# Rotations in four operations, and a state space core that gates one token tile per scan step

## What is computed

```python
def mamba2_mixer(u, w_in, ...):
    ...
    y = ssd_chunked_scan(xh * dt[..., None], dt * a, bm, cm)
    y = (y + xh * d_skip[:, None]).reshape(b, l, D_INNER)
    yg = (y * silu(z)).reshape(b, l, SSM_GROUPS, D_INNER // SSM_GROUPS)
    yg = yg * rsqrt(mean(square(yg), axis=-1, keepdims=True) + RMS_EPS)
    return (yg.reshape(b, l, D_INNER) * norm_w) @ w_out
```

```python
def rope(t):
    ...
    t1, t2 = t[..., :half], t[..., half:]
    return concatenate([t1 * cos - t2 * sin, t1 * sin + t2 * cos], axis=-1)
...
q, k, v = rope(hv(q)), rope(hv(k)), hv(v)
q_idx = rope(q_idx.reshape(B, S, IDX_HEADS, IDX_DIM))
k_idx = rope(k_idx[:, :, None, :])[:, :, 0, :]
...
sc = relu(einsum('bqhd,bsd->bqhs', q_idx_block, k_idx))
score = einsum('bqhs,bqh->bqs', sc, w_idx_block) * idx_scale
```

## Time and profile before

| | |
|---|---|
| median of three executions | 2491.34 us |
| lowest and highest | 2490.29, 2491.82 us |
| profiled execution | 2485.71 us |
| its span in the trace | 2484.0 us |
| granted TensorE clock, mean | 0.988 |
| TensorE busy | 2398.8 us, 97% |
| VectorE busy | 996.8 us, 40% |
| ScalarE busy | 636.3 us, 26% |
| GpSimd busy | 1497.5 us, 60% |

### The profile page before, as it was taken

How to read it: one execution, slowest core, us unless ns; L and a number is a source line. 1 busy time by engine, 2 the same in 40 slices (tenths; PEclk the granted TensorE clock), 3 DMA queues, 4 the chain that set the end, 5 groups by cost and what they waited for, 6 DMA issues and landing times.

```text
span 2484.0 us, 34378 instructions
## 1 busy us (share of the span) xinstructions
PE 2398.8 (97%) x14154; PEld 1942.6 (78%) x14154; DVE 996.8 (40%) x1582; ACT 636.3 (26%) x1303; POOL 1497.5 (60%) x1391
## 2 busy tenths in 40 slices
PE   8999999999999998999999999999798999999998
PEld 7887778888888886568888877666686788888887
DVE  3547662551251401435404346885532325311113
ACT  2224673020020114832101122255543211110010
POOL 7656777586685764428749747471122765765763
PEclk9999999999999999999999999999898999999999
DMA  5321114233232232113323213030000332332321
GB/s 167 93 85 43 52 57 152 89 111 102 81 107 93 94 102 78 27 34 120 102 68 126 95 54 109 28 111 18 2 4 20 105 94 77 118 94 85 106 86 63
DMA packets 106305, 201.79 MB, mean 81 GB/s; under 512 B 9530, under 2 KB 14628, under 8 KB 106148
## 3 DMA queue, kind: packets, MB, share of 16 engines
q1 hardware_dynamic: 101476, 189.36, 24.4%
q10 hardware_dynamic: 4672, 10.23, 1.3%
HBM read 194.71 MB, written 2.10 MB: 79 GB/s over the span
## 4 chain that ended last, share of the span: by engine, by line
PE 74%; DVE 5%; POOL 2%; ACT 2%; issue 1%; DVEq 0%; ACTq 0%; POOLq 0%
PE psum L160 31%; PE psum L304 24%; PE psum L162 4%; PE psum L242 3%; POOL weight_split_ring L446 1%; PE psum L1528 1%; PE psum L1536 1%; PE psum L204 1%; PE psum L1555 1%; DVE big L2131 1%; POOL weight_split_ring L443 1%; DVE best L2130 0%; PE psum L2443 0%; PE psum L2372 0%; ACT big L1588 0%
## 5 line engine op out<-in xcount | busy, mean ns | idle before, releaser
L446 POOL TENSOR_TENSOR weight_split_ring<-weight_ring,weight_split_ring 128x512 fp32r<-128x512 f32 (+3 forms) x732 | 959.7, 1331 | 30.6
L160 PE MATMUL psum<-x_split,weight_split_ring 128*128 128x512 f32 x4128 | 970.1, 393 | 2.9 <-DVE x_split L961 1.6
L160 PEld LDWEIGHTS psum<-x_split,weight_split_ring 128*128 128x128 f32 x4128 | 766.1, 187 | 174.4 <-issue 10.5
L443 POOL TENSOR_SCALAR weight_split_ring<-weight_ring 128x1024 fp32r<-128x1024 f32 (+3 forms) x366 | 395.9, 1082 | 593.2 <-PE psum L304 283.5
L304 PE MATMUL psum<-weight_split_ring,hidden_split 128*128 128x512 f32 x2256 | 514.1, 389 | 0.0
L304 PEld LDWEIGHTS psum<-weight_split_ring,hidden_split 128*128 128x128 f32 x2256 | 423.1, 188 | 87.4
L162 PE MATMUL psum<-weight_split_ring,x_split 128*128 128x512 f32 x864 | 220.1, 403 | 0.3 <-ACT big L1935 0.3
L162 PEld LDWEIGHTS psum<-weight_split_ring,x_split 128*128 128x128 f32 x864 | 158.1, 190 | 38.6 <-issue 7.4
L754 DVE TENSOR_TENSOR big<-big 128x512 f32<-128x512 f32 x64 | 86.7, 1355 | 179.0 <-ACT big L739 179.0
L739 ACT ACTIVATE big<-psum 128x512 f32<-128x512 f32 x64 | 38.3, 599 | 429.7 <-PE psum L160 372.9
L545 DVE SCALAR_TENSOR_TENSOR residual<-residual,psum 128x512 f32<-128x512 f32 x48 | 32.8, 683 | 220.1 <-PE psum L304 220.0
(11 more groups left out here) (367 smaller groups left out, 2564.5 us busy)
## 6 DMA issues: line engine op xcount, KB each, us to landing
weight_ring<-in_mlp_w SPq DMA_DIRECT2D x128, 512.0 KB, 3.7
weight_ring<-in_w_in SPq DMA_DIRECT2D x92, 512.0 KB, 3.6
weight_ring<-in_w_ffn_in SPq DMA_DIRECT2D x40, 512.0 KB, 3.7
weight_ring<-in_w_out SPq DMA_DIRECT2D x24, 512.0 KB, 3.8
weight_ring<-in_w_ffn_out SPq DMA_DIRECT2D x22, 512.0 KB, 3.7
weight_ring<-in_sb_w_q SPq DMA_DIRECT2D x8, 512.0 KB, 3.6
weight_ring<-in_sb_w_k SPq DMA_DIRECT2D x8, 512.0 KB, 3.6
weight_ring<-in_sb_w_v SPq DMA_DIRECT2D x8, 512.0 KB, 3.7
```

The costliest lines, as they stand in the source:

```text
L160: mm = pe.matmul(out, wp[:, k, m * P:m * P + rows], xp, start=first, stop=last)
L443: pool.tensor_scalar(part.high[:, 0:nk, 0:n], raw, 1.0, 0.0, ALU.mult, ALU.add).then_inc(self.high_made, 1)
L446: low = pool.tensor_tensor(part.low[:, k, 0:n], raw[:, k, :], part.high[:, k, 0:n].bitcast(F32), ALU.subtract)
```

## The change

The core gets four edits. Gates and squares handle one token tile in each of the four slots after `over[j]` for the first three pairs (`gating`); for the last pair all four token tiles are handled in slot 32. Inverse comes five slots after `over[j]` and normalise six, for the last pair both in slot 33 (`groups`). The turns begin seven slots after `over[j]`, for the last pair in slot 35 (`turns`), so seven of them stand behind slot 31 instead of five, at the positions 0, 1, 2 and 6 to 9 of `between` instead of 0 and 5 to 8. In ScalarE's queue the high parts now come behind squares, inverse and normalise of the same slot, and squares writes its unused result over the gate that was used, in SBUF, without the wait for `s_yl`.

The rotation is made of four operations on whole heads: x times sine into a scratch tile, x times cosine in place, and then the half heads are combined with one subtraction and one addition. The index queries are rotated two token tiles at a time, and each call waits for the second of them.

```diff
--- before.py
+++ after.py
@@ -1164,19 +1164,28 @@
     def before(self, pe, k):
         pe.wait_ge(self.s_yl, k)
 
-    def due(self, i, after):
-
-        return [(j, i - at - after) for j, at in enumerate(self.over) if i - at >= after]
+    def groups(self, i, after, end):
+
+        *early, last = range(len(self.over))
+        return [j for j in early if i == self.over[j] + after] + [last] * (i == self.STEPS + end)
+
+    def gating(self, i):
+
+        *early, last = range(len(self.over))
+        now = [(j, i - self.over[j] - 1) for j in early if 0 <= i - self.over[j] - 1 < NT]
+        return now + [(last, t) for t in range(NT) if i == self.STEPS]
 
     def turns(self, i):
 
-        return [NT * j + q for j, q in self.due(i, 5) if q < NT]
+        *early, last = range(len(self.over))
+        first = {j: self.over[j] + NT + 3 for j in early} | {last: self.STEPS + 3}
+        return [NT * j + i - at for j, at in first.items() if 0 <= i - at < NT]
 
     def between(self, pe, n, b, t):
 
         left = [k for i in range(self.STEPS, self.STEPS + 2 * NT) for k in self.turns(i)]
         at = 2 * b + t // 2 if n == 0 and t % 2 == 1 else None
-        late = [0] + list(range(5, 9))
+        late = [0, 1, 2] + list(range(6, 10))
         assert len(left) == len(late)
         if at in late:
             self.turn(pe, left[late.index(at)])
@@ -1278,13 +1287,11 @@
 
         def squares(j, t):
             act.wait_ge(self.s_gated, NT * j + t + 1)
-            if t == 0 and j >= 1:
-                act.wait_ge(self.s_yl, NT * j)
             for q in range(2):
                 n = 2 * (NT * j + t) + q
                 if n >= 2:
                     act.wait_ge(self.s_ss, n - 1)
-                act.activation(kit.psum[:, self.TURNS, q * self.GW:(q + 1) * self.GW], self.x(t, 2 * j + q), ACT.Square,
+                act.activation(self.gate(t)[:, q * self.GW:(q + 1) * self.GW], self.x(t, 2 * j + q), ACT.Square,
                                accum_out=m.gss[:, t, 2 * j + q:2 * j + q + 1]).then_inc(self.s_ss, 1)
 
         def inverse(j):
@@ -1311,16 +1318,14 @@
             if i == self.STEPS:
                 act.wait_ge(self.s_y, self.STEPS)
                 act.dma_start(m.h, self.a["x"].rearrange("b (t p) d -> (b p) t d", p=P)).then_inc(m.h_landed, 16)
+            for j, t in self.gating(i):
+                squares(j, t)
+            for j in self.groups(i, NT + 1, 1):
+                inverse(j)
+            for j in self.groups(i, NT + 2, 1):
+                normalise(j)
             for k in self.turns(i):
                 high(k)
-            for j, n in self.due(i, 1):
-                if n < 2:
-                    squares(j, 2 * n)
-                    squares(j, 2 * n + 1)
-                elif n == 2:
-                    inverse(j)
-                elif n == 3:
-                    normalise(j)
             if i == self.LAST_SILU:
                 for n in range(NT):
                     self.inlet.silu(act, self.inlet.first + n)
@@ -1409,10 +1414,8 @@
                 mix(i)
             if i in self.CONVOLVED:
                 self.inlet.conv(dve, self.inlet.first + self.CONVOLVED[i])
-            for j, n in self.due(i, 1):
-                if n < 2:
-                    gated(j, 2 * n)
-                    gated(j, 2 * n + 1)
+            for j, t in self.gating(i):
+                gated(j, t)
             for k in self.turns(i):
                 low(k)
 
@@ -2079,30 +2082,20 @@
     def vector(dve):
         step = kit.vector_chain(dve)
 
-        def rotate(t, x, n):
-            x = x.rearrange("p (h s d) -> p h s d", s=2, d=HD // 2)
-            x1, x2 = x[:, :, 0, :], x[:, :, 1, :]
-            cos, sin = (across(m.rope[:, t, q * 32:(q + 1) * 32], n) for q in range(2))
-            v = [m.rope_tmp[:, q, 0:n * 32].rearrange("p (h d) -> p h d", d=32) for q in range(2)]
-
-            step.mark(dve.tensor_tensor(v[0], x1, sin, ALU.mult))
-            step(dve.tensor_tensor(v[1], x2, sin, ALU.mult))
-            step.mark(dve.tensor_tensor(x1, x1, cos, ALU.mult))
-            step(dve.tensor_tensor(x2, x2, cos, ALU.mult))
-            step.mark(dve.tensor_tensor(x1, x1, v[1], ALU.subtract))
-            return dve.tensor_tensor(x2, x2, v[0], ALU.add)
-
-        def rotate_keys():
-            x1, x2 = (m.idxTok[:, :, ATT + 32 * q:ATT + 32 * q + 32] for q in range(2))
-            cos, sin = (m.rope[:, :, q * 32:(q + 1) * 32] for q in range(2))
-            v = [m.rope_tmp[:, q, 0:NT * 32].rearrange("p (t d) -> p t d", t=NT) for q in range(2)]
-
-            step.mark(dve.tensor_tensor(v[0], x1, sin, ALU.mult))
-            step(dve.tensor_tensor(v[1], x2, sin, ALU.mult))
-            step.mark(dve.tensor_tensor(x1, x1, cos, ALU.mult))
-            step(dve.tensor_tensor(x2, x2, cos, ALU.mult))
-            step.mark(dve.tensor_tensor(x1, x1, v[1], ALU.subtract))
-            return dve.tensor_tensor(x2, x2, v[0], ALU.add)
+        def rotate(t0, x, heads):
+
+            nt = x.shape[1]
+            x = x.rearrange("p t (g d) -> p t g d", d=HD // 2)
+            cos, sin = (m.rope[:, t0:t0 + nt, q * 32:(q + 1) * 32].unsqueeze(2).broadcast_to([P, nt, 2 * heads, 32])
+                        for q in range(2))
+            v = m.rope_tmp[:, :, :].rearrange("p q c -> p (q c)")[:, 0:nt * heads * HD]\
+                 .rearrange("p (t g d) -> p t g d", t=nt, d=HD // 2)
+
+            step.mark(dve.tensor_tensor(v, x, sin, ALU.mult))
+            step(dve.tensor_tensor(x, x, cos, ALU.mult))
+            x1, x2 = x[:, :, 0::2, :], x[:, :, 1::2, :]
+            step.mark(dve.tensor_tensor(x1, x1, v[:, :, 1::2, :], ALU.subtract))
+            return dve.tensor_tensor(x2, x2, v[:, :, 0::2, :], ALU.add)
 
         def add_term(i):
             t, hp, n = pair(i // 2)
@@ -2159,12 +2152,12 @@
         mu0 = m.col0["mu"]
         dve.tensor_scalar(m.rest_mu, m.par_cols[:, 0, mu0:mu0 + RW_COLS // P], -1.0, 1.0, ALU.mult, ALU.add).then_inc(s_mu, 1)
         dve.wait_ge(s_cs, 16)
-        for t in range(NT):
-
-            gi.wait_free(dve, t)
-            step(rotate(t, m.idxTok[:, t, 0:ATT], NHEAD))
+        for t in range(0, NT, 2):
+
+            gi.wait_free(dve, t + 1)
+            step(rotate(t, m.idxTok[:, t:t + 2, 0:ATT], NHEAD))
         dve.wait_ge(s_tf, 1)
-        step(rotate_keys())
+        step(rotate(0, m.idxTok[:, :, ATT:ATT + HD], 1))
         dve.tensor_copy(m.widx[:, :, :], m.idxTok[:, :, ATT + HD:IDXW]).then_inc(s_rot, 1)
         for i in range(STEPS):
             add_term(i)
@@ -2178,7 +2171,7 @@
             if t >= 1:
 
                 dve.wait_ge(s_rq, t)
-            rotate(t, m.qkTok[:, t, :], 2 * NHEAD).then_inc(s_rq, 1)
+            rotate(t, m.qkTok[:, t:t + 1, :], 2 * NHEAD).then_inc(s_rq, 1)
         choose(2, CHOICE[0], last=False)
         shift(0)
         shift(1)
```

## The result

The changed kernel takes 2497.09 us (median of 18 runs, 2493.84 to 2502.77), the kernel before 2490.64 beside it: the ratio is 1.0031, with an interval of 1.0024 to 1.0038. The ratio is an estimate from all the runs and not the quotient of the two medians, which is 1.0026; the means differ by 7.6 us. By the medians it is 6.5 us more, where 2.1 were forecast: inside the range of 2484.5 to 2499, but above the 0.2% that counted as no change, so the likeliest case, "no change that shows", lost to the side that had 0.22. The profiled execution took 2494.86 us (span 2493.2), 9.2 more than the profiled one of before.

What follows compares the result with a forecast made beforehand. TensorE, at 74% of the chain, was taken as the bound, so only its waits count. Rotations -8.2, scan -0.5 and end of scan +10.8 sum to +2.1 us on the median 2491.34: 2493.4 us, range 2484.5 to 2499.

Steps and rivals of the forecast that it cites:

- no change that shows: Whole kernel: the summed change stays within 5 us of zero; chance 0.62.
- the side that had 0.22: Whole kernel: measurably slower, by more than the 0.2% (5 us) a measurement can tell; chance 0.22.
- Rotations, -8.2 forecast: Ahead of the index transposes: TensorE's 5.48 us wait goes, and 2.8 us more come back from the clock.
- The other bound: Index rotations: 1024-column operations take 2.6 us, `s_rot` comes half a microsecond late, gain 7.7 us instead of 8.2.
- Rival B: Slots 18 to 20 and 25 to 27: gate plus low part overfill VectorE's hole, +4.8 us, total 2498; chance 0.22.
- ScalarE: [...] nothing: Inside the scan: squares into SBUF, later inverse, normalise and turns, and the dropped `s_yl` wait cost nothing.
- part 3: End of the scan: TensorE waits ahead of turns 10 and 11, +10.8 us, ends +8 and +12.5.
- part 2: Core inside the scan: gates and low parts in VectorE's holes sum to -0.5 us, ends -3 and +5.
- first group's gain: Scan slots 11 to 14: one gate per slot instead of two gains 0.75 of a 0.86 us wait.
- The 1.5 for the clock: End of the scan: slower matmuls after the second stall cost 1.5 us, ends 0 and 3.
- C: End of the scan: last gates run undisturbed, +10.8 becomes +6; total about 2486 us; chance 0.11.
- D: End of the scan: no stall, since the queue order was misread; -8.7 us, 2482.6 us; chance 0.05.

Runs made afterwards that it cites:

- experiment 3: Six narrow operations for attention's queries and keys: in the rotations-alone kernel, ratio 0.9960 against 0.9979; in the changed kernel, 1.0018 against 1.0031.
- experiment 6: Changed kernel with ScalarE's high parts ahead of squares, inverse and scaling in slots 0 to 31: 2490.39 us, ratio 0.9999 to the kernel before, scan 183.1 us.
- experiment 4: Changed kernel, turns' parts moved forward from slot 32: ahead of that slot's work, ratio 1.0015; between the last pair's pieces, 0.9993, both to the kernel before.
- experiment 5: Changed kernel, pairs 0 to 2 partly undone: two tiles per slot again, ratio 1.0025; gates, inverse, scaling and turns at old slots, 0.9980, both to kernel before.
- interleaved kernel: Changed kernel with the parts of turns 9 to 11 placed between the last pair's gates and squares: ratio 0.9993 to the kernel before, end 61.2 us.
- turns' parts first: Changed kernel, from slot 32 high parts ahead of squares, inverse and scaling, low parts ahead of gates: ratio 1.0015 to kernel before, end 65.9 us.

## Why the prediction was right, and where it was wrong

- **Rotations, -8.2 forecast, -8.64 in their stretch.** Right in each step: no wait, clock 1.00, 2.2 us from the twelve matmuls and 0.5 from the first transposes; the four transposes at today's L1805 gave 0.26 more (0.70 to 0.44), which I hadn't counted. VectorE was ready 2.6 us ahead of TensorE and not 0.8. That isn't the work of the 1024-column operations, though they took 1.47 and 2.07 us and not 2.4 each, since the keys had to wait for ScalarE's copy anyway; the four operations of the keys took 3.8 us and not 6. The other bound, worked out from the lock for a whole instruction in the Trainium skill ("SBUF — State Buffer", "Who interferes with whom"), was too dear: by it VectorE would have been late. The estimate took each operation to wait for a whole GpSimd instruction. Both engines' lengths are what a lock gives when one starts within the other's instruction: VectorE's lie between 1.22 us alone and 2.6, and GpSimd's instructions beside them grew as well (the high part from 1.05 to 2.04 us, the two low parts from 2.55 to 3.83). The masks fit it best: the selection that starts together with a rotation ends 0.5 us behind it, whichever its width (experiment 3). So the trace contradicts my estimate of 2.6 us and not the rule; which part of the overlap is the lock is argued, not shown.
- **Queries, keys and GpSimd, nothing forecast, +1.3 in the trace.** The step that failed is "well ahead of the transposes that read them: nothing": I looked at who reads the result, not at who works beside it. The sentence that GpSimd is chunks ahead was true of the index rotations and not of this place, where it has just made masks for 16 us and is on the edge: before, the chunk was cut at 1618.13 and wanted at 1618.34. The wait for line 446 that the prediction names as the sign is what appeared.
- **Scan, -0.5 forecast, +2.56 measured.** Rival B's place was right (slots 18 to 20 and 25 to 27), its mechanism wrong. B had the gate and the low part overfill VectorE's hole; experiment 6 has the same gates and low parts in the same slots and is 6 us faster. The step that failed is "ScalarE: [...] nothing". The order "squares, then high part" was read from the diff and used in part 3 for the end of the scan, but not in part 2, though it is the same loop. With the order put back the scan is 3.4 us shorter than before, and the order costs 6.0: my -0.5 stood for two terms of which one was far too small and the other missing. What is left of B's mechanism there is at most the 1.3 us of waits for the fold. The first group's gain was also over-sized, 0.3 us and not 0.75 (a wait of 1.07 us at 274.89, in slot 13, where I had said none over 0.5).
- **End of the scan, +10.8 forecast, +10.03 measured.** Right in its waits: turn 10 begins 10.8 us behind the first product of `mix1` (10.4 forecast), turn 11 17.9 (17.65), waits of 4.62 and 0.98 (4.4 and 1 to 4), clock 0.50 after the first. What I hadn't seen is which part of it matters: undone by order alone (experiment 4), and absent with only one turn left over (experiment 5). The 1.5 for the clock were nothing: the slow twelve matmuls end ahead of turn 11's release, and the 48 behind it take 11.28 us, the full pace (11.29 in the interleaved kernel, with no stall of that size before them). Where a single stall of 3.81 us stands right ahead of those 48, as with the turns' parts first, they take 12.54. Rivals C and D fall with the rows above: the four gates took 6.6 us beside GpSimd, and the queues were read rightly.
- **The sum**, +2.1 forecast, +6.5 measured. The forecast missed 3.1 us in the scan and 1.3 at the masks, and had 0.4 and 0.8 too much in the other two, which makes the 5.2 of the traces up to rounding. That the total stayed inside the range is in part luck: of the scan's missing 6.0 us, 3 were given back by the gain that I had too small. The last 1.2 (2.4 by the means) I can't place. Three other profiles of this core have a scan 1.5 to 2.1 us longer than the one used here, each with a lower clock somewhere in it (last section), so it may be that; this is argued, not shown.

Not tried: whether the squares' output in SBUF instead of PSUM, and the wait that went with it, cost or gain anything. With the order put back, no slot of the scan from 14 on is more than 0.3 us longer than before.

## What to carry to other kernels

When operations of several jobs share an in-order queue, put those that have their inputs already (a turn's high part) ahead of those that wait for another engine (squares behind a gate); 0.67 us of work behind such a wait held up two other engines here, and the repair was a move of two lines. Read a reordering in the diff in every place where its loop runs, not only where the effect is largest. An edit that makes VectorE's operations wider has to be costed at whoever of GpSimd's clients is on the edge beside it, and idle time of TensorE at more than its length: filling 5.5 us of it with useless matmuls was worth some 3 us.

## What the runs showed that I had not expected

The granted clock after the same idle time differs from one execution to another. Ahead of the second normalisation TensorE waits 2.54 us in both profiled runs; before, then after:

```profile
2113.53 3.13 PE L242 MATMUL psum<-x_split,weight_split_ring 128*128 128x256 f32 x24 [2.54 <-DVE x_split L535]
```

```profile
2121.22 4.63 PE L242 MATMUL psum<-x_split,weight_split_ring 128*128 128x256 f32 x24 [2.54 <-DVE x_split L535]
```

Of the fourteen profiles, thirteen have 4.5 to 4.6 us here; only the profiled execution of before has 3.13. It was a fast one: its 2485.71 us lie below all eighteen runs of that kernel beside the changed one (2487.80 to 2491.82). So the two profiled executions differ by more than the kernels do.

Behind a wait of 1.81 us in slot 20 of the scan, six matmuls take 1.63 us in the changed kernel and 2.79 in the kernel with the turns' parts first, whose core is the same up to there:

```profile
321.02 1.63 PE L162 MATMUL psum<-weight_split_ring,x_split 128*128 128x512 f32 x6
```

```profile
320.88 2.79 PE L162 MATMUL psum<-weight_split_ring,x_split 128*128 128x512 f32 x6
```

So a wait of this size costs its length in one execution and 1.5 us more in another. This is why the scan took 189.1 and 189.0 us in two profiles and 190.7, 190.7 and 191.2 in three others with the same core up to slot 31; each of the three has a clock of 0.50 somewhere in the scan, the two have none. It may also be why the order of ScalarE (experiment 6) brought 8 us by the ratios and 6 in the trace; that last step is argued, not shown. It also sets the spread of a kernel: eight executions of the rotations alone went from 2480.5 us at a mean clock of 0.988 to 2487.0 at 0.984. One profiled execution is no measure for terms of 1 or 2 us; the same matmul's place in two traces is, up to the first such difference.
